# Moving the half swap of rotary embeddings from TensorE to transfers issued by GpSimd, in a two-block fp32 layer stack on one Trainium2 core

## The reference, cut to what matters

```python
def apply_rope(x, cos, sin):
    half = x.shape[-1] // 2
    x1 = x[..., :half].astype(F32)
    x2 = x[..., half:].astype(F32)
    c = cos[:, :, None, :]
    s = sin[:, :, None, :]
    return jnp.concatenate([x1 * c - x2 * s, x2 * c + x1 * s], axis=-1).astype(x.dtype)
...
q_nsa  = partial_rope(...)   # the first 16 of 64 dims of each head
k_pe   = apply_rope(...)     # 32 dims, shared by the five latent heads
q, k   = apply_rope(...)     # retention: all 64 dims
q2, k2 = apply_partial_rope(...)  # second block: 16 of 64 dims, 8 + 8 heads
```

## Time and profile before

| | us |
|---|---|
| median of three runs | 1517.23 (1515.48 to 1518.75) |
| the profiled execution | 1515.29 |
| its span (first to last instruction) | 1513.5 |
| PE busy / PEld busy | 1481.1 / 1441.9 |
| DVE busy | 1085.0 |
| ACT busy | 783.4 |
| GpSimd busy | 63.3 |

### The profile page before, as it was taken

The page is one execution under the profiler, slowest core; times in us unless marked ns, Lnnn a source line. Parts: engine busy times, 40 slices in busy tenths (PEclk is TensorE's granted clock), DMA queues, the critical chain, the costliest instruction groups (busy, mean ns, idle before and its releaser), DMA issues.

```text
span 1513.5 us, 29309 instructions
## 1 busy us (share of the span) xinstructions
PE 1481.1 (98%) x12148; PEld 1441.9 (95%) x12148; DVE 1085.0 (72%) x1931; ACT 783.4 (52%) x1370; POOL 63.3 (4%) x73
## 2 busy tenths in 40 slices
PE   8999999999999999999999999999999999999999
PEld 8888999999888999999999989999999999999999
DVE  8777788887777788788884577665569646766653
ACT  6555577435555487434555545444444554454442
POOL 0000000000000000000030030000003003100000
PEclk9999999999999999999999999999999999999999
DMA  8233389886234378887444444555434434454551
GB/s 327 80 142 121 142 308 341 325 335 259 101 113 167 140 265 328 325 341 271 165 161 149 168 143 151 197 179 195 173 144 158 168 141 167 139 194 170 194 184 67
DMA packets 42435, 296.56 MB, mean 196 GB/s; under 512 B 5056, under 2 KB 5312, under 8 KB 6848
## 3 DMA queue, kind: packets, MB, share of 16 engines
q1 hardware_dynamic: 41888, 294.67, 53.5%
q10 hardware_dynamic: 416, 0.02, 0.0%
HBM read 293.62 MB, written 1.05 MB: 195 GB/s over the span
## 4 chain that ended last, share of the span: by engine, by line
PE 74%; DVE 12%; DMA 6%; ACT 4%; issue 2%; POOL 1%; SPq 0%; DVEq 0%; ACTq 0%
PE acc L771 22%; PE acc L772 21%; PE acc L773 21%; DMA ring<-stream 6%; DVE wL L1688 5%; ACT wH L1333 2%; PE ps_t L898 1%; DVE ring L1678 1%; PE ps_s L885 1%; PE ps_o L908 1%; PE ps_o L907 1%; PE ps_s L883 1%; PE acc L972 1%; PE acc L867 1%; POOL region L2419 1%
## 5 line engine op out<-in xcount | busy, mean ns | idle before, releaser
L1688 DVE TENSOR_TENSOR wL<-ring,wH 128x1024 fp32r<-128x1024 f32 x444 | 548.5, 1242 | 276.8 <-ACT wH L1333 272.2
L771 PE MATMUL acc<-hH,wH 128*128 128x256 f32 x2240 | 648.0, 289 | 7.7 <-DVE wL L1688 3.2
L773 PE MATMUL acc<-hH,wL 128*128 128x256 f32 x2240 | 633.5, 283 | 0.0
L772 PE MATMUL acc<-hL,wH 128*128 128x256 f32 x2240 | 633.5, 283 | 0.0
L1333 ACT ACTIVATE wH<-ring 128x1024 fp32r<-128x1024 f32 x444 | 461.7, 1050 | 224.6 <-DMA ring<-stream 122.1
L771 PEld LDWEIGHTS acc<-hH,wH 128*128 128x128 f32 x2240 | 429.2, 192 | 14.0 <-issue 8.6
L772 PEld LDWEIGHTS acc<-hL,wH 128*128 128x128 f32 x2240 | 429.4, 192 | 3.5 <-issue 2.6
L773 PEld LDWEIGHTS acc<-hH,wL 128*128 128x128 f32 x2240 | 429.1, 192 | 0.0
L771 PE MATMUL acc<-aH,wH 128*128 128x256 f32 x864 | 245.4, 284 | 3.2 <-DVE wL L1688 3.2
L772 PE MATMUL acc<-aL,wH 128*128 128x256 f32 x864 | 244.5, 283 | 0.0
L773 PE MATMUL acc<-aH,wL 128*128 128x256 f32 x864 | 244.4, 283 | 0.0
(11 more groups left out here) (326 smaller groups left out, 1720.3 us busy)
## 6 DMA issues: line engine op xcount, KB each, us to landing
ring<-stream SPq DMA_DIRECT2D x276, 1024.0 KB, 4.9
cst<-consts SPq DMA_DIRECT2D x1, 1363.0 KB, 16.1
x<-xin SPq DMA_DIRECT2D x4, 256.0 KB, 3.7
out<-x SPq DMA_DIRECT2D x4, 256.0 KB, 4.2
onc<-once SPq DMA_DIRECT2D x1, 516.0 KB, 16.5
v1all<-vec SPq DMA_DIRECT2D x1, 355.0 KB, 8.9
v2all<-vec SPq DMA_DIRECT2D x1, 330.0 KB, 17.8
nv<-pos SPq DMA_DIRECT2D x1, 256.0 KB, 3.7
```

Of the source, the lines that this page charges most:

```text
L771: pe.matmul(out, w[0], y[0], start=first, stop=False)
L772: pe.matmul(out, w[0], y[1], start=False, stop=False)
L773: return pe.matmul(out, w[1], y[0], start=False, stop=last)
L1688: TTN(wL[:, n % SPLIT, :], ring[:, g % RING, half * UNIT:(half + 1) * UNIT], wH[:, n % SPLIT, :].bitcast(F32), ALU.subtract).then_inc(lo_r ...
```

## The change

Three of the twelve rotations of a first-block layer (q0, ks, q1) keep the matrix product. For the other nine (`SWAPPED1`) and for the four of a second-block layer, GpSimd issues four DMAs each that copy one half of the rotated rows onto the partitions of the other half, from `raw` to a new buffer `swapped` (three slots, used in turn), or from `qk2` to `swapped2` (two slots). Rows that are not rotated stay zero by a memset at the start of a layer, which their sine table makes irrelevant. The sign sits in the sine tables (`inv` negated for the first half of the rows), and the matrix `rotp` loses its minus sign. GpSimd's copies of the latent query weights (`queries_copied`) move behind the third swap. On DVE the rotations of slot i now stand behind `feed`, `scores` and `output`. The rotation entries leave the order of the PSUM banks. GpSimd issues the four second-block swaps of a layer ahead of the window sums.

```diff
@@ order1 / order2
     for i in range(SLOTS1):
-        out += ["rot_" + u for u in MID1.get(i, []) if u[:2] != "mq"]
         out += [fill1(i)] if fill1(i) else []
...
-        if i in ROTATE_AT:
-            out.append(f"rotp{ROTATE_AT[i]}")
@@ constants
-                m[s + half + i, s + i] = -1.0
+                m[s + half + i, s + i] = 1.0
...
+    for s in (0, 64):
+        inv[s:s + 8, 0], inv[s:s + 32, 2], inv[s:s + 8, 3] = -inv[s:s + 8, 0], -inv[s:s + 32, 2], -inv[s:s + 8, 3]
+    inv[64:80, 1] = -inv[64:80, 1]
@@ TensorE
-                        project(u, hs, mid=lambda: middle(i))
+                        project(u, hs)
...
-                    if i in ROTATE_AT:
-                        b = ROTATE_AT[i]
-                        pe.wait_ge(qn2_ready, L * 4 + (b + 1))
-                        a = open_acc(f"rotp{b}")
-                        pe.matmul(a[:, :], C("rotp"), qk2[:, 2 * b:2 * b + 2, :], start=True, stop=True).then_inc(acc_full, 1)
@@ VectorE, rope
-                a = full(tn, "rot_" + name, L)
-                TTN(ts[rows, :], a[rows, 0:S], trig[rows, 1, tab, :], ALU.mult)\
-                    .then_inc(acc_drained[tn.bank("rot_" + name)], 1)
+                if name in SWAPPED1:
+                    at = L * len(SWAPPED1) + SWAPPED1.index(name)
+                    dve.wait_ge(swap_in[at % SWAPS], 64 * (at // SWAPS + 1))
+                    link(TTN(ts[rows, :], swapped[rows, at % SWAPS, :], trig[rows, 1, tab, :], ALU.mult))
@@ VectorE, slots
-                    for u in MID1.get(i, []):
-                        rope1_block(u)
                     if i == 6:
                         shifted(raw[:, RAW1["vc"], :], 1)
...
                     if i >= 2:
                         output(i - 2)
+                    for u in MID1.get(i, []):
+                        rope1_block(u)
@@ GpSimd, first block
+            def swap(dst, src, half, starts, signal):
+
+                for r, cols in starts:
+                    for at, to in ((r + half, r), (r, r + half)):
+                        dma(dst[to:to + half, cols], src[at:at + half, cols]).then_inc(signal, 16)
...
+                for n, u in enumerate(SWAPPED1):
+                    at = L * len(SWAPPED1) + n
+                    if u == "kpe":
+                        queries_copied(L)
+                        pool.wait_ge(acc_drained[A1.bank(u)], A1.drained(u, L))
...
+                    if n >= SWAPS:
+                        pool.wait_ge(rope_ready, L * len(ROPES1) + ROPES1.index(SWAPPED1[n - SWAPS]) + 1)
+                    dst, src = swapped[:, at % SWAPS, :], raw[:, RAW1[u], :]
+                    swap(dst, src, 16 if u == "kpe" else (32 if u[0] == "r" else 8),
+                         by_columns if u == "kpe" else every64, swap_in[at % SWAPS])
@@ GpSimd, second block
+                for b in range(4):
+                    at = L * 4 + b
+                    pool.wait_ge(qn2_ready, at + 1)
+                    if b >= 2:
+                        pool.wait_ge(qk2_ready, at - 1)
+                    swap(wide(swapped2[at % 2]), wide(qk2[:, 2 * b:2 * b + 2, :]), 8, every64, swap2_in[at % 2])
```

More of the change, by code:

```diff
@@ L193 @@
         11: ["rkb", "mq2"], 12: ["r4", "mq3"], 13: ["mq4"]}
+SWAPPED1 = [u for i in range(SLOTS1) for u in MID1.get(i, []) if u[:2] != "mq"]
+SWAPS = 3
 ROPES1 = ["q0", "ks", "q1"] + [u for i in range(SLOTS1) for u in MID1.get(i, [])]
@@ L487, in trn_kernel @@
         gnst = piece(6, 10)
+        swapped = piece(SWAPS, S)
         cursor[0] = 0
@@ L498, in trn_kernel @@
         cv = piece(2, 2 + S)
+        swapped2 = [piece(2, S) for _ in range(2)]
         cursor[0] = 0
@@ L596, in trn_kernel @@
         uq_ready = sem("uq_ready")
+        zeroed = sem("zeroed")
+        swap_in, swap2_in = [sem(f"swap_in{i}") for i in range(SWAPS)], [sem(f"swap2_in{i}") for i in range(2)]
         ge = sem("ge")
@@ L932, in rotated @@
                 def rotated(u):
-                    if u[:2] == "mq":
-                        return
                     drained(u)
[L937 to L941, removed]
+                    rotate(u, C("rotp"), raw[:, RAW1[u], :])
                 def roped(u):
@@ L1805, in rope @@
                 TTN(tc[rows, :], src, trig[rows, 0, tab, :], ALU.mult)
-                a = full(tn, "rot_" + name, L)
-                TTN(ts[rows, :], a[rows, 0:S], trig[rows, 1, tab, :], ALU.mult)\
-                    .then_inc(acc_drained[tn.bank("rot_" + name)], 1)
-                dve.wait_ge(acc_drained[tn.bank("rot_" + name)], tn.drained("rot_" + name, L))
+                if name in SWAPPED1:
+                    at = L * len(SWAPPED1) + SWAPPED1.index(name)
+                    dve.wait_ge(swap_in[at % SWAPS], 64 * (at // SWAPS + 1))
+                    link(TTN(ts[rows, :], swapped[rows, at % SWAPS, :], trig[rows, 1, tab, :], ALU.mult))
+                else:
+                    a = full(tn, "rot_" + name, L)
+                    TTN(ts[rows, :], a[rows, 0:S], trig[rows, 1, tab, :], ALU.mult)\
+                        .then_inc(acc_drained[tn.bank("rot_" + name)], 1)
+                    dve.wait_ge(acc_drained[tn.bank("rot_" + name)], tn.drained("rot_" + name, L))
                 for dst, part in outs:
@@ L2266, in _ @@
                         TTN(tcs[:], qk2[:, 2 * b:2 * b + 2, :], pair(trig[:, 0, 3, :]), ALU.mult)
[L2267 to L2271, removed]
+                        at = L * 4 + b
+                        dve.wait_ge(swap2_in[at % 2], 64 * (at // 2 + 1))
+                        link(TTN(tss[:], swapped2[at % 2], pair(trig[:, 1, 3, :]), ALU.mult))
                         TTN(qk2[:, 2 * b:2 * b + 2, :], tcs[:], tss[:], ALU.add).then_inc(qk2_ready, 1)
@@ L2384, in _, with queries_copied @@
             nc.gpsimd.memset(one[:], 1.0).then_inc(one_ready, 1)
-            for L in range(LAYERS):
+            dma = nc.gpsimd.dma_start
+            def swap(dst, src, half, starts, signal):
+                for r, cols in starts:
+                    for at, to in ((r + half, r), (r, r + half)):
+                        dma(dst[to:to + half, cols], src[at:at + half, cols]).then_inc(signal, 16)
+            every64 = [(r, slice(0, None)) for r in (0, 64)]
+            by_columns = [(64, slice(c, c + P)) for c in (0, P)]
+            def queries_copied(L):
                 g = tile_of(1, L, TILES1.index(("small", 0)))
                 pool.wait_ge(got[g % RING], 16 * (g // RING + 1))
-                if L > 0:
-                    pool.wait_ge(acc_full, A1.full(f"dn{KC - 1}", L - 1))
                 uq = ring[:, g % RING, UQ:UQ + 960].rearrange("p (c h n) -> p c h n", c=2, h=MLA_HEADS)
@@ L2397, in _ @@
             for L in range(LAYERS):
+                if L > 0:
+                    pool.wait_ge(acc_full, A1.full(f"dn{KC - 1}", L - 1))
+                nc.gpsimd.memset(swapped[:, :, :], 0.0).then_inc(zeroed, 1)
+                pool.wait_ge(zeroed, L + 1)
+                for n, u in enumerate(SWAPPED1):
[3 more added lines that the diff above has]
+                        pool.wait_ge(acc_drained[A1.bank(u)], A1.drained(u, L))
+                    else:
+                        pool.wait_ge(acc_drained[A1.bank(u)], A1.drained(u, L))
+                    if n >= SWAPS:
[3 more added lines that the diff above has]
+                         by_columns if u == "kpe" else every64, swap_in[at % SWAPS])
+            for L in range(LAYERS):
                 own[0] = 0
                 pool.wait_ge(pad_ready, L + 1)
+                for b in range(2):
+                    last = nc.gpsimd.memset(swapped2[b], 0.0)
+                link(last)
+                wide = lambda v: v.rearrange("p a s -> p (a s)")
+                for b in range(4):
+                    at = L * 4 + b
+                    pool.wait_ge(qn2_ready, at + 1)
+                    if b >= 2:
+                        pool.wait_ge(qk2_ready, at - 1)
+                    swap(wide(swapped2[at % 2]), wide(qk2[:, 2 * b:2 * b + 2, :]), 8, every64, swap2_in[at % 2])
                 w0 = 16
```

7 lines of the change are left out of this document (2 added, 5 removed).

## The result

The changed kernel takes 1527.49 us in the median of 20 runs (1511.36 to 1545.26), the kernel before 1515.31 us (1511.76 to 1521.77, 20 runs). The ratio is 1.0064 with a 95% interval of 1.0050 to 1.0077: slower by 0.64%. The forecast was 1514.0 us, in a range of 1503 to 1527.

The account below looks back on a forecast made before the run. TensorE was taken to bound the kernel (three quarters of the chain). Second-block gain -6.8, its waits +1.2 and the first block +2.4 gave -3.2 us: 1517.23 to 1514.0 us, range 1503 to 1527.

Parts of the forecast that it names:

- TensorE's savings: Rotations taken off TensorE: 7.7 us in the first block, 6.8 in the second, together 14.5 us at most.
- `hidk`: First block, slot 5: TensorE would wait for DVE ahead of it, 1 to 1.6 us, in both layers.
- the opening of `r4`'s bank: First block, slot 11: TensorE would wait about 2 us for DVE to release the bank of `kcc`, both layers.
- `ct`: First block, slot 13: it would run at 125.0 instead of 123.82, TensorE waiting about 1.2 us, both layers.
- 6.8 - 1.2 = 5.6 us: Second block: TensorE gains 6.8 us, less a wait at `pw1` taken as 0.6 us in each layer.
- GpSimd's window sums: Second block: they would start near 763 (763.8 after four issues) and end within 1.3 us of `pw1`.
- `pw`: Second block: TensorE would wait 0 to 1.3 us at `pw1` for the window sums, taken as 0.6, per layer.
- the term "+2.4" for the first block: First block: waits net of the nine rotations saved cost 1.2 us in a layer, 2.4 us in two.
- the sum: Whole kernel: -6.8 + 1.2 + 2.4 = -3.2 us, from 1517.23 to 1514.0 us.
- Rival 1: First block, slots 6 to 12: DVE catches up, saving up to 7.7 us; 1504 us, or 1509 for half; chance 0.20.
- Rival 2: First block, slots 3 and 4: swaps for q2 and kc come late, over 6.5 us each; 1523 us; chance 0.35.
- price of a swap: GpSimd's DMAs: 1.0 us per issue and 3.2 to land, so ready 6.2 us after its copy.

Follow-up runs that it names:

- run 9: Changed kernel with six dummy matmuls (results unread) in `ct`'s bank ahead of the wait for `ct`'s input, both layers; 1514.43 us, ratio 1.0000 to the kernel before.
- run 4: Kernel before, all rotations on TensorE, with only VectorE's order changed: rotations' products behind feed, scores and output; 1524.32 us, ratio 1.0057.
- run 1: Changed kernel without its GpSimd DMAs, sine products reading zeroed swap buffers, order kept on every engine; 1532.06 us, ratio 1.0055 to the kernel before.
- run 8: Changed kernel with VectorE's order of before, the rotations' products first in each slot; 1546.81 us, ratio 1.0206 to the kernel before.
- run 3: Changed kernel with two dummy matmuls (results unread) where each of the first block's nine rotations stood on TensorE; 1529.26 us, ratio 1.0076 to the kernel before.
- run 6: Changed kernel with the second block's rotations back on TensorE, so swaps by DMA in the first block alone; 1533.63 us, ratio 1.0114 to the kernel before.
- run 7: Changed kernel with `kcc` and `mq3` changing places in TensorE's order of slot 10, giving `r4` another bank; 1523.67 us, ratio 1.0028 to the kernel before.
- run 2: Changed kernel with four dummy matmuls (results unread) where each of the first block's nine rotations stood; 1527.90 us, ratio 1.0098 to the kernel before.
- run 12: Kernel before with two scratch products on VectorE ahead of the compressed weights, delaying `ct`'s input, both layers; 1533.63 us, ratio 1.0151.

## Why the prediction was wrong

**What it had right.** TensorE's savings and the waits came out place by place. `hidk` was to wait 1 to 1.6 us and waited 1.3 and 1.4; the opening of `r4`'s bank about 2 and waited 2.1; `ct` about 1.2 and waited 1.2, in both layers. The second block was to gain 6.8 - 1.2 = 5.6 us and gained 5.4. GpSimd's window sums started at 782.2, which on the clock of the kernel before is 762.3 (the second block's first sum of squares starts 747.3, before 727.4), where 763.8 was said; `pw` waited 0.3 to 0.4 us per layer of the 0 to 1.3 allowed. The term "+2.4" for the first block, taken without the clock, measured 2.6.

**Where it failed.** In the term "+2.4" for the first block, and there at `ct`: "net of the nine rotations: +1.2 us in a layer". The wait was priced at its own length. It had a second price, TensorE's clock at 1.2 GHz for some 30 us behind it, 13.6 us in the profiled run, in 17 of 20 runs at least once. The prediction named three waits of TensorE in a stretch that had none over 0.6 us, and asked of each only how long it was. Neither the sum nor a rival had a term for the clock; every row that it was made from was read at 1.00.

Run 9 has the same three waits with the one at `ct` filled, and takes 1514.43 us where the sum said 1514.0. That match is luck: the sum started from 1517.23 us, and the kernel before took 1515.02 beside run 9. The sum forecast a gain of 3.2 us; run 9's ratio of 1.0000 shows none, within 2.6 us either way. The two short falls in its profile can account for about 3.4 us (3.4 us each at half the clock, an estimate), so the short falls behind waits are a second thing that the sum left out.

**The rivals.** Rival 1 (the rotations come back whole) fell: run 4 shows that the order on VectorE costs 9 us and eats them. With the waits at `ct` filled and the one at `r4` taken away, 1506.2 is reached, 0.46% under the kernel before, most of it the second block's 5.4 us. Rival 2 (swaps late at q2 and kc) gave nearly the measured time, 1523, by a mechanism that was not at work: run 1 has no swaps and is as slow. The prediction's price of a swap was too high too: 0.51 us per issue where 1.0 was taken, 2.0 to land where 3.2 was, together 3.5 us for 6.2. By the Trainium skill (DMA: Bandwidth & Descriptors, "Anatomy of one DMA — SWDGE (gpsimd) path") about 2.0 us was to be expected, and the medians of 1.7 to 2.0 agree; the 5.8 us that `r4`'s DMAs took in their median beside the stream of weights do not. The other rule of the Trainium skill that the prediction cited (SBUF — State Buffer, "Who interferes with whom") left nothing to see, since issues took 0.48 to 0.69 us throughout. Late swaps exist, as run 8 shows, but at `kpe` and `r4` and only without the new order.

**The chances.** "Slower" had 0.36, all but a little of it for rival 2, which was not the reason; where that chance came true, it was by luck. The range ended at 1527, half a microsecond under the median.

**What stays open.** Why the wait at `ct` matters so much more than others was not tried. A wait of 1.2 us there, or of 0.7 to 0.8 in run 3, was followed by a long fall in most runs, but not in all: in the first layer of the changed kernel's own profile the same wait brings none. One of 2.1 us at `r4` was followed by a short fall or by none, three of 0.8 to 1.4 us in run 4 by none, and one of 1.1 us in slots 16 and 17 of the kernel before, with other short waits around it, by none. What TensorE does around these places differs, but no run here varied that. So a long fall behind a short wait is shown for `ct` alone.

## What to carry to other kernels

A new wait on TensorE is not priced by its length alone: where the clock row was full before, hold a fall of the clock behind that wait as a rival with a price of its own (13.6 us here for a wait of 1.2), and do not take the length of the wait for its risk. When a kernel gets slower by more than its waits add up to, compare the granted clock over many runs before looking for a culprit among the new instructions, and try matmuls that nothing reads, in the bank that is opened anyway: six per layer took back the loss here. When an order is changed to hide a latency, time the order by itself.

## What the runs showed of the hardware that was not expected

- TensorE's granted clock, in a program on one core that is 97% busy, falls from 2.4 to 1.2 GHz behind a wait of 0.7 to 1.2 us at `ct`, for 30.7 to 34.1 us in the profiles of the changed kernel and of runs 3, 6 and 7, though TensorE is busy nearly throughout. The Trainium skill (TensorE: Matmul & The Clock Gate, "HAM oscillation — how this bites in real kernels") names longer gaps than these as what lets the clock fall. Run 8, where it falls inside waits of 4.1 and 3.7 us, agrees with that; the falls behind `ct` do not.
- Falls come short, 3.4 us, and long, 30.7 to 37.5 us. The short ones stand behind waits of 1.5 to 2.4 us: at `r4` (runs 1, 6 and 9), for the stream of weights (run 9), and ahead of the slots near 29 us (runs 2, 4 and 7, a wait of 1.9 us where the kernel before waits 1.5 without a fall). Neither kind comes in every execution: long ones came in 5 of 6 in run 12.
- A GpSimd DMA of 8 to 32 KB inside SBUF took 0.51 us to issue and 1.7 to 2.0 us to land; four of 32 KB each took 5.8 us in the median while the weights were streamed.
- The stage of up and down products between the slots and the layer's end varies from run to run: 217.0 to 222.8 us in the first layer, over the profiles in which no fall reaches into it and which are the same there. One profile cannot tell a gain of 3 us in it.
